# A hybrid two-layer decoder: the high and low parts of one PSUM bank's products in one 512-column matmul, and two weight sums made by accumulating transfers

## The reference

```python
D_MODEL, SEQ, DEPTH, D_FF = 1024, 512, 2, 2816

def swiglu(h, w_gate_up, w_down):
    gu = h @ w_gate_up
    g, u = gu[..., :D_FF], gu[..., D_FF:]
    return (jax.nn.silu(g) * u) @ w_down

def reference(x, mem, ...):
    h = x
    for layer in range(DEPTH):
        h = h + mixer(rmsnorm(h, mix_norm), ...)
        h = h + memory_cross_attention(rmsnorm(h, ...), rmsnorm(mem, ...), ...)
        h = h + swiglu(rmsnorm(h, ffn_norm[layer]), ffn_w_gate_up[layer], ffn_w_down[layer])
    return rmsnorm(h, final_norm)
```

## Time and profile before

| | |
|---|---|
| median of 3 runs | 1380.35 us (1379.12 to 1381.93) |
| the profiled execution | 1380.13 us, of it 1378.4 us span |
| busy: TensorE, VectorE, ScalarE, POOL | 99%, 73%, 49%, 10% of the span |
| granted TensorE clock, mean | 0.998 |

### The profile page before, as it was taken

How to read it: one execution, slowest core, us unless ns; L and a number is a source line. 1 busy time by engine, 2 the same in 40 slices (tenths; PEclk the granted TensorE clock), 3 DMA queues, 4 the chain that set the end, 5 groups by cost and what they waited for, 6 DMA issues and landing times.

```text
span 1378.4 us, 22076 instructions
## 1 busy us (share of the span) xinstructions
PE 1367.0 (99%) x8608; PEld 1229.4 (89%) x8608; DVE 1000.5 (73%) x1335; ACT 678.4 (49%) x1000; POOL 140.1 (10%) x107
## 2 busy tenths in 40 slices
PE   9999999999999999999999999999999999999997
PEld 7988888889999998998887888988888999998997
DVE  5756556469877879995668855755558977888995
ACT  5633434355454456353756635534455454556342
POOL 0012200110000000231111211100020000000031
PEclk9999999999999999999999999999999999999999
DMA  8732221224332335354221212542031523224342
GB/s 316 283 96 73 98 91 42 91 78 121 111 107 95 121 108 138 108 171 165 92 92 47 77 47 77 182 154 77 32 106 62 153 93 121 94 98 142 100 151 77
DMA packets 44159, 154.59 MB, mean 112 GB/s; under 512 B 5280, under 2 KB 5792, under 8 KB 43936
## 3 DMA queue, kind: packets, MB, share of 16 engines
q1 hardware_dynamic: 38592, 136.79, 28.8%
q0 software_dynamic: 1728, 6.29, 2.5%
q10 hardware_dynamic: 3744, 10.17, 2.0%
HBM read 151.14 MB, written 2.10 MB: 111 GB/s over the span
## 4 chain that ended last, share of the span: by engine, by line
PE 90%; DVE 6%; issue 1%; DMA 1%; ACT 1%; SPq 0%; ACTq 0%; POOLq 0%; POOL 0%; DVEq 0%
PE acc L2312 15%; PE acc L2314 15%; PE acc L2313 15%; PE acc L2635 8%; PE acc L2637 8%; PE acc L2636 8%; PE acc L2360 2%; PE acc L2362 2%; PE acc L2361 2%; PE aux L2686 2%; PE aux L2689 1%; PE aux L2688 1%; PE acc L2686 1%; PE acc L2689 1%; PE acc L2688 1%
## 5 line engine op out<-in xcount | busy, mean ns | idle before, releaser
L1389 DVE TENSOR_TENSOR w_lo<-raw,w_hi 128x1024 fp32r<-128x1024 f32 (+1 forms) x149 | 181.9, 1222 | 99.6 <-ACT w_hi L701 99.2
L701 ACT ACTIVATE w_hi<-raw 128x1024 fp32r<-128x1024 f32 (+1 forms) x149 | 152.7, 1028 | 78.2 <-PE acc L2314 38.6
L2312 PE MATMUL acc<-u_hi,w_hi 128*128 128x512 f32 x352 | 138.7, 394 | 0.0
L2314 PE MATMUL acc<-u_hi,w_lo 128*128 128x512 f32 x352 | 137.2, 390 | 0.0
L2313 PE MATMUL acc<-u_lo,w_hi 128*128 128x512 f32 x352 | 137.1, 389 | 0.0
L2635 PE MATMUL acc<-b_hi,s_hi 128*128 128x256 f32 x432 | 122.4, 283 | 0.0
L2637 PE MATMUL acc<-b_hi,s_lo 128*128 128x256 f32 x432 | 122.3, 283 | 0.0
L2636 PE MATMUL acc<-b_lo,w_hi 128*128 128x256 f32 x432 | 122.3, 283 | 0.0
L2636 PE MATMUL acc<-b_lo,s_hi 128*128 128x256 f32 x432 | 122.3, 283 | 0.0
L2637 PE MATMUL acc<-b_hi,w_lo 128*128 128x256 f32 x432 | 122.2, 283 | 0.0
L2635 PE MATMUL acc<-b_hi,w_hi 128*128 128x256 f32 x432 | 122.2, 283 | 0.0
(11 more groups left out here) (332 smaller groups left out, 3835.8 us busy)
## 6 DMA issues: line engine op xcount, KB each, us to landing
raw<-in_weights SPq DMA_DIRECT2D x253, 512.0 KB, 3.4
raw<-in_weights POOLq DMA_DIRECT2D x8, 512.0 KB, 5.5
hT<-in_x_t ACTq DMA_DIRECT2D x4, 512.0 KB, 5.5
x_tok<-in_x ACTq DMA_DIRECT2D x4, 512.0 KB, 5.4
memT<-in_weights POOLq DMA_DIRECT2D x4, 512.0 KB, 5.6
raw<-in_weights SPq DMA_DIRECT2D x5, 256.0 KB, 5.6
mem_tok<-in_mem ACTq DMA_DIRECT2D x2, 512.0 KB, 8.1
memT<-in_mem_t ACTq DMA_DIRECT2D x1, 1024.0 KB, 5.7
```

Source lines behind the costliest of these rows:

```text
L701: act.activation(w_hi[:, s, c], raw[:, s, c], ACT.Copy).then_inc(hi_ready, 1)
L1389: dve.tensor_tensor(w_lo[:, s, c], raw[:, s, c], w_hi[:, s, c].bitcast(F32), ALU.subtract)\
L2312: pe.matmul(out, w_h, x_h, start=first, stop=False)
L2314: return pe.matmul(out, w_l, x_h, start=False, stop=last)
```

## The change

From pair 4 on (FIRST), the products 1, 6, 5 and 3 (MERGED), which share a bank, take the high and the low part of the input in one matmul of 512 columns: the high part's result goes to the bank's first half, the low part's to its second half, and the third matmul (low weights by high input) still has 256 columns and goes to the first half. b_hi and b_lo become two halves of one buffer, b_both. What was one region is now two halves that have to be added:

- copies 1 and 6 (ScalarE) copy 512 columns in place of 256;
- each of the three quarters (VectorE) has a second add, of the low half, which waits for the first;
- the last quarter, which gate_second and up_second had read straight out of the region, is made by two new steps: low_copy (ScalarE, copies the low half after product 3) and twelve (VectorE, adds it). gate_second moves behind copy 6 and reads twelve's result; up_second waits for twelve.

Of the four weight sums, VectorE keeps two: pair_sums (POOL) loads one block into pair_pre (half of memT, which is idle here) and adds a second block to it by an accumulating transfer, and adds a block to the one in raw by another. pair_hi waits for the latter in place of VectorE's sum, first_sums for the former. As one summand now lies in memT, sum_hi and sum_lo are two instructions each. The small buffers for copy 7 and low_copy lie in sqsum. POOL's transfers for the down projection come behind those of pair_sums. The transfers of a pair carry three blocks of 128x512 (256 KB).

```diff
+FIRST = 4
+MERGED = (1, 6, 5, 3)
...
-        b_hi = at("b_hi", 80, [P, 7, 4, S // 2], F32R)
+        b_both = at("b_both", 80, [P, 2, 7, 4, S // 2], F32R)
+        b_hi, b_lo = b_both[:, 0], b_both[:, 1]
...
+                def low_copy(q):
+
+                    act.wait_ge(product_done, product_at(layer, q, 3))
+                    if q > FIRST or layer:
+                        act.wait_ge(twelve_ready, low_at(layer, q) - 1)
+                    act.activation(pair_low, bank_a(q)[:, half(1)], ACT.Copy).then_inc(low_copied, 1)
...
                 for q in range(PAIRS):
                     last = q == PAIRS - 1
-                    if q % 2:
+                    if q > FIRST:
+                        low_copy(q - 1)
+                    elif q % 2:
                         gate_second(q - 1)
                     copy_product(q, 6)
+                    if q > FIRST and q % 2:
+                        gate_second(q - 1)
                     if not last:
                         sum_hi(q + 1)
...
+            def pair_sums(layer, q):
+
+                n, k = pair_unit(layer, q), nth(layer, q)
+                pool.wait_ge(prod_ready, PLAIN * (layer + 1))
+                if q >= FIRST + 2:
+                    pool.wait_ge(slo_ready, PAIRS * layer + q - 1)
+                pool.dma_start(pair_pre(q), d["weights"][n + 1, :, 0:512]).then_inc(first_sum_in[q % 2], 16)
+                pool.wait_ge(raw_in[(n + 1) % RING], 16 * ((n + 1) // RING + 1))
+                pool.dma_start(raw[:, (n + 1) % RING, 512:1024], d["weights"][n, :, 0:512], accum_op=ALU.add)\
+                    .then_inc(third_sum_in[q % 2], 16)
+                pool.wait_ge(first_sum_in[q % 2], 32 * k - 16)
+                pool.dma_start(pair_pre(q), d["weights"][n + 1, :, 512:1024], accum_op=ALU.add)\
+                    .then_inc(first_sum_in[q % 2], 16)
...
-                    part, copy = {11: (region_c(q), copy_1), 21: (region_e(q), copy_u), 22: (region_a(q), copy_7)}[c]
-                    dve.tensor_tensor(dst, part, copy, ALU.add).then_inc(quarter_ready, 1)
+                    part, copy = {11: region_c(q), 21: region_e(q), 22: region_a(q)}[c], pair_copy(q, of)
+                    ins = dve.tensor_tensor(dst, part, copy[:, 0:S // 2], ALU.add)
+                    if c == 22 and merged(q, 5) or c != 22 and merged(q, of):
+                        low = bank_a(q)[:, half(1)] if c == 22 else copy[:, half(1)]
+                        i = step(ins)
+                        dve.wait_ge(dve_step, i)
+                        ins = dve.tensor_tensor(dst, dst, low, ALU.add)
+                    ins.then_inc(quarter_ready, 1)
+
+                def twelve(q):
+
+                    dve.wait_ge(low_copied, low_at(layer, q))
+                    dst = tmp[:, 0, half(1)] if q % 2 == 0 else act_f[:, PLAIN + q - 1, half(1)]
+                    if q % 2 == 0:
+                        dve.wait_ge(up_ready, third_at(layer, q - 1, 3))
+                    dve.tensor_tensor(dst, region_a(q), pair_low, ALU.add).then_inc(twelve_ready, 1)
...
                 for q in range(PAIRS):
                     last = q == PAIRS - 1
+                    if q > FIRST:
+                        twelve(q - 1)
                     if q and q % 2 == 0:
                         up_second(q - 1)
...
+                        if merged(q, m):
+                            pe.matmul(bank_a(q)[:, :], hi[:, w], b_both[:, :, STEP_B[m], k, :], start=first, stop=False,
+                                      skip_group_check=True)
+                        else:
+                            pe.matmul(out, hi[:, w], x_h, start=first, stop=False, skip_group_check=True)
+                            pe.matmul(out, hi[:, w], x_l, start=False, stop=False, skip_group_check=True)
                         ins = pe.matmul(out, lo[:, w], x_h, start=False, stop=(k == 3), skip_group_check=True)
```

More of the change, by code:

```diff
@@ L360, in program @@
         s3_ready = sem("s3_ready")
+        first_sum_in = [sem(f"first_sum_in{e}") for e in range(2)]
+        third_sum_in = [sem(f"third_sum_in{e}") for e in range(2)]
+        low_copied = sem("low_copied")
+        quarter_low = sem("quarter_low")
+        twelve_ready = sem("twelve_ready")
         s_ready = sem("s_ready")
@@ L491, in pair_cols, with pair_pre, nth, merged @@
             return ring[:, n:n + 2, :]
+        def pair_pre(q):
+            return mem_flat[:, q % 2 * 512:q % 2 * 512 + 512]
+        pair_7, pair_low = sqsum[:, 0:S // 2], sqsum[:, S // 2:S]
+        def nth(layer, q):
+            return (PAIRS // 2 - 2) * layer + q // 2 - 1
+        def merged(q, m):
+            return q >= FIRST and m in MERGED
+        def low_at(layer, q):
+            return (PAIRS - FIRST) * layer + q - FIRST + 1
+        def pair_copy(q, m):
+            if m == 7:
+                return pair_7
+            return tmp[:, 2 if m == 1 else 3, 0:S if merged(q, m) else S // 2]
+        def bank_a(q):
+            return accs[2 * (q % 2)]
         def region_a(q):
-            return accs[2 * (q % 2)][:, 0:S // 2]
+            return bank_a(q)[:, 0:S // 2]
         def region_c(q):
@@ L931, in gate_second @@
                 def gate_second(q):
-                    act.wait_ge(product_done, product_at(layer, q, 3))
-                    act.activation(tmp[:, 0, half(1)], region_a(q), ACT.Silu).then_inc(gate_ready, 1)
+                    if q >= FIRST:
+                        act.wait_ge(twelve_ready, low_at(layer, q))
+                        src = tmp[:, 0, half(1)]
+                    else:
+                        act.wait_ge(product_done, product_at(layer, q, 3))
+                        src = region_a(q)
+                    act.activation(tmp[:, 0, half(1)], src, ACT.Silu).then_inc(gate_ready, 1)
                 def act_hi_part(c):
@@ L1366, in _ @@
                     norm_power(norm)
+                for q in range(FIRST, PAIRS):
+                    pair_sums(layer, q)
                 down_sums(layer)
@@ L1749, in first_sums @@
                         dve.wait_ge(product_done, product_at(layer, q - 2, 5))
+                    if q >= FIRST:
+                        dve.wait_ge(first_sum_in[q % 2], 32 * nth(layer, q))
+                        return step(dve.tensor_tensor(sums[:, 1, :], pair_pre(q), raw[:, x, 0:512], ALU.add))
                     i = step(dve.tensor_tensor(sums[:, 0, :], raw[:, y, 0:512], raw[:, y, 512:1024], ALU.add))
```

36 lines of the change are left out of this document (26 added, 10 removed).

## The result

The changed kernel takes 1388.92 us (median of 6 runs, 1388.18 to 1394.42) against 1380.53 of before (6 runs): 1.0069 of it, 95% interval 1.0053 to 1.0084, so 8.4 us slower where 6.3 were forecast. The profiled execution has a span of 1386.3 us.

What follows compares the result with a forecast made beforehand. The prediction took TensorE, its number of matmuls times their pitch, as the bound. Saving 5.8 us and losing 12.1 to late products gave +6.3 us, 1386.6 us in the median shown, range 1379 to 1394.

Steps and rivals of the forecast that it cites:

- listed signs: Right: pitch 0.227 in the pairs, TensorE waiting about 1 us in odd pairs; wrong: VectorE waiting for memT by DMA.
- What the change takes away: TensorE in the pairs: 448 matmuls fewer, each merge saving 0.013 us, 5.8 us in all.
- Even iteration: Even pairs: quarter 22 ready at 8.39, TensorE starts product (q, 3) at 8.54 against 8.48, late by 0.06 us.
- Odd iteration: Odd pairs: twelve waits for low_copy behind pair_hi, product (q, 3) late by 1.03 us, pair 5 by about 0.55.
- The second add: VectorE's quarters: an add that reads its predecessor's result starts 0.45 us after it, not 0.34; a quarter takes 0.79.
- Rival two: VectorE's dependent add costs only 0.34, odd pairs late by 0.31: 1377.7 us, 0.2% faster; chance 0.13.
- The transfers, costed at nothing: POOL's three transfers per pair: landing from two us early to half a us late at double size, so no cost.
- The half should be quicker: POOL's transfers of 256 KB should land sooner than the 512 KB rows, accumulations of 5.5 and 7.3 to 7.9 us.
- rival three: The chained transfers into pair_pre arrive after first_sums wants them: 12 us per us late, 1398 at one us; chance 0.08.
- Behind the last pair, costed at nothing: After the pairs: chain to the last act_lo some 3.7 us, covered by TensorE's 24 matmuls of 5.4 us, so nothing.
- Sum: Whole kernel: -5.8 + 12.1 = +6.3 us, giving 1386.6 us, slower by 0.45%.

Runs made afterwards that it cites:

- the matmuls alone: The kernel before with only the merged matmuls, low-part products of 1, 6, 5 and 3 left out of the result: 1376.78 us, 0.9978 of before.
- twelve late: The changed kernel with twelve and up_second behind pair_lo in VectorE's queue, gate_second behind sum_hi in ScalarE's: 1379.97 us, 0.9999 of before.
- gate_tile late: The changed kernel with gate_tile of even pairs from pair 4 moved into the next iteration, directly ahead of gate_second: 1384.75 us, 1.0036 of before.
- the transfers in time: four buffers and POOL's order added together: 1377.74 us on twelve late, 1379.23 us on gate_tile late.
- four buffers: pair_pre with four buffers in place of two, added to twelve late (1386.74 us) or to gate_tile late (1387.97 us).
- POOL's order: pair_pre's accumulation issued before POOL's wait for the raw unit; on twelve late 1396.35 us with two buffers, 1377.74 us with four buffers.

## Why the prediction was right

The direction, the place and nearly every time in the chains came out: TensorE waits before product (q, 3) of odd pairs for the second add of quarter 22, because VectorE waits for low_copy at the head of the iteration. ScalarE's pair_hi, as foreseen, starts 1.3 us later on the even iteration's clock (9.5 after product 6's issue; 8.2 before). Two of the listed signs did not fit: the pitch in the pairs is 0.235 and not 0.227, and VectorE did wait for memT, a sign of being wrong, though off the path that decides. By its steps:

- **What the change takes away**: mis-sized. 0.013 us per merge was taken from a row of uniform 512-column matmuls; in the mix a merge saves 0.007, 3.0 us in all (the run with the matmuls alone), not 5.8.
- **Even iteration**: 0.06 late was forecast; the trace has about 0.10, nearly all of it the longer first matmul of (q, 3) (421.12 to 421.46 is 0.34 in place of 0.24).
- **Odd iteration**: 1.03 late was forecast; the trace has 0.90 in five pairs, and 0.4 in pair 5 (forecast 0.55). Counted from product 6's issue at about 422.6, twelve starts at 2.0 (forecast 2.03) and quarter 22 is ready at 9.3 (forecast 9.36). The difference is on TensorE's side: merged products of 1.41 us want product 3 at 8.56 and not 8.48. The stages' 185.45 less the 180.09 of the matmuls alone give 5.4 per layer, 10.7 us in both, for the forecast 12.1.
- **The order, and not the amount of work**, is the cause: the runs with twelve late and with gate_tile late, both with the transfers in time, do the same work in stages of 180.1 and 180.4.
- **The second add** costs 0.45 before what follows on it (420.19 to 420.64 in the trace). Rival two is out. The Trainium skill ("VectorE: DVE Perf Modes", "The DRAIN you can't avoid") says that a semaphore after each operation costs nothing extra; this trace disagrees, with 0.45 to an add that waits for its predecessor (428.53 to 428.98) against 0.34 to one that does not (428.19 to 428.53).
- **The transfers, costed at nothing**: right for the sum, but two things were overlooked. "The half should be quicker" came out: the accumulation into raw lands in 3.7 us in the median (5.5 for 512 KB), the one into memT in 5.5 (7.3 to 7.9). What the prediction took for the accumulation's wait was its own load; in the trace POOL stood 28 times, for 111.7 us in all, before the accumulation into raw for SP's load, and before the one behind it for its own load only three times, for 1.3 us. And the prediction counted the time from an even iteration alone, where by its clocks VectorE wants the sum 11.6 us after the load's issue. From an odd one it is less: the sum whose load was issued at 410.95 was wanted at 421.06, 10.1 us later, and came 0.58 late. The change got away with it because VectorE would have been waiting for low_copy at that time. Once that wait was cured, rival three's mechanism appeared: four buffers and POOL's order together were worth 2.2 us with twelve late and 5.5 with gate_tile late, and the order by itself 9.0 where the buffers had made it worse.
- **Behind the last pair, costed at nothing**: failed. It followed the chain to act_lo, which had cover, and not what stands behind twelve and up_second in VectorE's queue for the down projection, which took 0.34 us longer in the first layer and 1.2 in the second. The 0.34 also stand in a trace without these steps, so only the second layer's part is likely theirs.
- **Sum**: -3.0 + 10.7 + 1.5 = +9.2. The changed kernel's profiled execution also reached the pairs 1.4 us earlier (328.01 for 329.37) for reasons outside the change: most of it is one wait of 0.8 us for a weight's low part at 27.25 us of before, which no other trace shows. That leaves 7.8 of the 7.9 us by which the span is longer. The forecast of 6.3, for a measured 8.4, is as near as it is partly by luck: it took the gain 2.8 too large and left out 1.5, and a loss 1.4 too large made up for some of it.

## What to carry to other kernels

An engine's queue is a list of waits in order: a short new step at its head that waits for another engine delays everything behind it, so put a step that waits behind the long step that doesn't, if its own reader has time. The same holds for a queue that only issues transfers. Before calling a transfer hidden, find out what hides it: if it is a wait that you mean to remove, the transfer is next. And a term of a sum should come from a row with the same neighbours, not only of the same shape.

## What the runs showed of the hardware

- The matmul behind a 512-column one that alternates with 256-column ones starts 0.235 us after it, and the one behind the 256-column one 0.118 (means of 212 distances each from 370 to 508 us of the changed kernel); uniform rows are 0.227 and 0.120. Contiguous columns or two runs 28 KB apart make no difference (stages of 180.08 and 180.09).
- TensorE's first matmul after it waited is some 0.10 us longer than its kind (0.50 for 0.40 at 411.06).
- How long an accumulating transfer of 256 KB takes to land depends on what is under way beside it. In the changed kernel the one into raw, issued when SP's load had just landed, takes 3.7 us, and the one into memT, issued some 0.6 us behind it, 5.5:

```profile
L1382 POOL DMA_DIRECT2D raw<-in_weights x28: 841/852/881, 350.1 to 1232.2; - x28
...
DMA to landing us min/median/max: 3.6/3.7/5.4
```

```profile
L1385 POOL DMA_DIRECT2D memT<-in_weights x28: 842/1174/1214, 350.7 to 1232.8; - x28
...
DMA to landing us min/median/max: 4.7/5.5/6.9
```

With the two in the other order and two buffers the first, now the one into memT, takes 4.3 and the second 6.9. With four buffers and the order the one into memT goes out before SP's load has landed (POOL waits for that load next, 28 times) and takes 5.8. One of 512 KB into raw takes 5.3 to 5.5.
- SP's plain loads of 512 KB landed in 3.9 us in the median before and in 5.8 in the changed kernel, in the stretch from 380 to 500 us, beside these transfers. There, by the table of DMA queues, POOL's transfers keep the DMA engines busy 1.8 times as long per byte as SP's (packets, MB, share of the 16 engines' time):

```profile
q0 software_dynamic: 4314, 9.68, 41.6%
q1 hardware_dynamic: 3171, 11.54, 27.1%
```
